# Attention loop of a hybrid attention trunk: the order of the exponential and the copy of the transposed probabilities on ScalarE

## What is computed

```python
def _masked_softmax(s, mask, axis):
    s = jnp.where(mask, s, NEG_INF)
    m = jnp.max(s, axis=axis, keepdims=True)
    e = jnp.where(mask, jnp.exp(s - m), 0.0)
    return e / jnp.maximum(jnp.sum(e, axis=axis, keepdims=True), 1e-30)
...
        ps = _masked_softmax(ss, ms[:, :, None], (-2, -1))
        o_s = jnp.einsum('bgrtkl,bgtkld->btgrd', ps.astype(dt), vs)
...
        pw = _masked_softmax(sw, mw, -1)
        o_w = jnp.einsum('bgrts,bsgd->btgrd', pw.astype(dt), vw)
        return gb[..., 0:1] * o_c + gb[..., 1:2] * o_s + gb[..., 2:3] * o_w
```

## Time and profile before

| what | value |
|---|---|
| median of 3 runs | 2489.19 us (2485.69 to 2492.6) |
| the profiled execution, its own time | 2496.24 us |
| span of its instructions | 2494.1 us |
| mean granted TensorE clock | 0.983 of full speed |
| PE busy | 2335.1 us, 94% of the span |
| ACT busy | 576.9 us, 23% |
| DVE busy | 1435.8 us, 58% |
| POOL busy | 1333.2 us, 53% |

### The profile page before, as it was taken

One profiled execution on the slowest core, in us unless ns is written; L12 is line 12 of the kernel. 1 busy time (PEld: TensorE's weight loads), 2 busy tenths in 40 slices (PEclk: granted clock), 3 DMA queues, 4 the chain that ended last, 5 costly groups with the idle time before them and its releaser, 6 DMA issues.

```text
span 2494.1 us, 36305 instructions
## 1 busy us (share of the span) xinstructions
PE 2335.1 (94%) x12736; PEld 1875.6 (75%) x12736; DVE 1435.8 (58%) x2460; ACT 576.9 (23%) x1114; POOL 1333.2 (53%) x1018
## 2 busy tenths in 40 slices
PE   0798999999999999999998999999999999999996
PEld 0566787877788877777886788787778888787885
DVE  8965654665677775675126155246677776335536
ACT  0211310222233333222024022022232232333001
POOL 6574447544444445555655644654544444554763
PEclk9998999998999999999999999999999999999998
DMA  9855336521122223454315533532222222221532
GB/s 351 307 210 193 121 135 230 172 102 61 67 69 68 72 73 110 155 202 156 100 63 195 197 99 103 184 121 94 69 69 71 73 69 68 69 82 62 193 135 93
DMA packets 94593, 315.92 MB, mean 127 GB/s; under 512 B 10918, under 2 KB 11174, under 8 KB 93382
## 3 DMA queue, kind: packets, MB, share of 16 engines
q1 hardware_dynamic: 86768, 295.46, 34.5%
q10 hardware_dynamic: 7644, 18.16, 2.1%
HBM read 303.86 MB, written 8.39 MB: 125 GB/s over the span
## 4 chain that ended last, share of the span: by engine, by line
PE 70%; DVE 15%; ACT 4%; POOLq 3%; issue 3%; DMA 2%; POOL 2%; DVEq 1%; ACTq 1%; SPq 0%
PE bank L653 14%; PE bank L655 14%; PE bank L654 13%; DVE arena L1715 9%; PE bank L1177 4%; PE bank L1176 4%; PE bank L1175 4%; DVE acc L1715 3%; ACT arena L1205 2%; PE bank L963 2%; PE bank L934 1%; PE bank L617 1%; POOLq L1657 1%; POOL w_lo L1655 1%; DVE tiny L1715 1%
## 5 line engine op out<-in xcount | busy, mean ns | idle before, releaser
L1655 POOL TENSOR_TENSOR w_lo<-ring,w_hi 128x512 fp32r<-128x512 f32 (+1 forms) x632 | 894.5, 1436 | 48.5 <-issue 1.3
L1651 POOL CAST w_hi<-ring 128x1024 fp32r<-128x1024 f32 (+1 forms) x320 | 356.4, 1114 | 1029.9 <-PE bank L655 844.6
L653 PE MATMUL bank<-h_hi,w_hi 128*128 128x512 f32 x1952 | 818.2, 419 | 9.3 <-POOLq L1657 9.3
L655 PE MATMUL bank<-h_hi,w_lo 128*128 128x512 f32 x1952 | 768.3, 394 | 0.0
L654 PE MATMUL bank<-h_lo,w_hi 128*128 128x512 f32 x1952 | 765.5, 392 | 0.0
L653 PEld LDWEIGHTS bank<-h_hi,w_hi 128*128 128x128 f32 x1952 | 370.9, 190 | 91.8 <-issue 15.0
L655 PEld LDWEIGHTS bank<-h_hi,w_lo 128*128 128x128 f32 x1952 | 368.8, 189 | 82.7
L654 PEld LDWEIGHTS bank<-h_lo,w_hi 128*128 128x128 f32 x1952 | 371.0, 190 | 72.5 <-issue 7.2
L1205 ACT ACTIVATE arena<-bank 128x512 f32<-128x512 f32 (+5 forms) x324 | 155.4, 480 | 660.0 <-PE bank L655 217.1
L1715 DVE SCALAR_TENSOR_TENSOR acc<-yT,cact,acc 128x1024 f32<-128x1024 f32 (+1 forms) x144 | 213.2, 1480 | 38.7 <-DMA acc<-in_b_mod 14.7
L1175 PE MATMUL bank<-w_hi,h_hi 128*128 128x512 f32 x448 | 175.7, 392 | 0.8 <-issue 0.8
(11 more groups left out here) (232 smaller groups left out, 2848.0 us busy)
## 6 DMA issues: line engine op xcount, KB each, us to landing
ring<-in_stream SPq DMA_DIRECT2D x352, 512.0 KB, 3.4
yT<-in_stream SPq DMA_DIRECT2D x128, 512.0 KB, 4.6
yT<-in_mod SPq DMA_DIRECT2D x32, 1024.0 KB, 7.8
arena<-in_x ACTq DMA_DIRECT2D x4, 1024.0 KB, 10.3
x_norm<-arena ACTq DMA_DIRECT2D x4, 1024.0 KB, 8.2
arena<-x_norm ACTq DMA_DIRECT2D x4, 1024.0 KB, 10.9
out<-arena SPq DMA_DIRECT2D x3, 1024.0 KB, 3.9
arena<-in_x SPq DMA_DIRECT2D x1, 2048.0 KB, 14.5
```

Source lines behind the costliest of these rows:

```text
L653: mm(PJ[b][:, :], hi, h_hi[:, k, :], start=(k == 0), stop=False)
L655: last = mm(PJ[b][:, :], lo, h_hi[:, k, :], start=False, stop=(k == KT - 1))
L1651: pool.tensor_copy(w_hi[:, par, 0:w], ring[:, slot, 0:w])
L1655: pool.tensor_tensor(w_lo[:, par, at], ring[:, slot, at], w_hi[:, par, at].bitcast(F32), ALU.subtract)
```

## The change

In the loop over the steps of a head, on ACT, the copy of the transposed probabilities of unit s-2 now stands ahead of the exponential of unit s-1. Nothing else differs; the waits, the operands and the semaphores are the same.

```diff
                             if s == 0:
                                 act.wait_ge(S("cmp_scored2"), H + 1)
                                 fn(cmp_s, cmp_s, ACT.Exp).then_inc(S("cmp_exp"), 1)
+                            if 2 <= s <= 9:
+                                u = s - 2
+                                w = (u % TT + 1) * P
+                                act.wait_ge(S("pt_done"), H * 8 + u + 1)
+
+                                act.wait_ge(S("pv_done"), after("pv_done", H * 8 + max(u - 1, 0)))
+                                fn(probT[u % 2][:, 0:w], TB[(u + 1) % 2][:, 0:w], ACT.Copy)\
+                                    .then_inc(S("pt_ready"), 1)
                             if 1 <= s <= 8:
                                 u = s - 1
                                 w = (u % TT + 1) * P
                                 act.wait_ge(S("max_ready"), H * 8 + u + 1)
                                 fn(prob[u % 2][:, 0:w], SB_[(u + 1) % 2][:, 0:w], ACT.Exp, scale=-1.0,
                                    bias=tiny[:, u:u + 1], accum_out=tiny[:, 8 + u:9 + u]).then_inc(S("exp_done"), 1)
-                            if 2 <= s <= 9:
-                                u = s - 2
-                                w = (u % TT + 1) * P
-                                act.wait_ge(S("pt_done"), H * 8 + u + 1)
-
-                                act.wait_ge(S("pv_done"), after("pv_done", H * 8 + max(u - 1, 0)))
-                                fn(probT[u % 2][:, 0:w], TB[(u + 1) % 2][:, 0:w], ACT.Copy)\
-                                    .then_inc(S("pt_ready"), 1)
```

More of the change, by code:

```diff
@@ L1403, in group @@
                                 fn(cmp_s, cmp_s, ACT.Exp).then_inc(S("cmp_exp"), 1)
-                            if 1 <= s <= 8:
-                                u = s - 1
-                                w = (u % TT + 1) * P
-                                act.wait_ge(S("max_ready"), H * 8 + u + 1)
-                                fn(prob[u % 2][:, 0:w], SB_[(u + 1) % 2][:, 0:w], ACT.Exp, scale=-1.0,
-                                   bias=tiny[:, u:u + 1], accum_out=tiny[:, 8 + u:9 + u]).then_inc(S("exp_done"), 1)
                             if 2 <= s <= 9:
@@ L1417, in group @@
                                     .then_inc(S("pt_ready"), 1)
+                            if 1 <= s <= 8:
+                                u = s - 1
+                                w = (u % TT + 1) * P
+                                act.wait_ge(S("max_ready"), H * 8 + u + 1)
+                                fn(prob[u % 2][:, 0:w], SB_[(u + 1) % 2][:, 0:w], ACT.Exp, scale=-1.0,
+                                   bias=tiny[:, u:u + 1], accum_out=tiny[:, 8 + u:9 + u]).then_inc(S("exp_done"), 1)
                             if g == KVH - 1 and r == GROUP - 1 and s == 9:
```

## The result

The changed kernel took 2494.44 us in the median of 20 runs (2489.82 to 2504.59), the kernel before 2490.56 us in 20 runs on the same chip (2484.99 to 2494.81). The ratio is 1.0020 with a 95% interval of 1.0011 to 1.0029: slower by 0.2%, some 5 us, or 3.9 us by the medians. The forecast was 2.8 us slower, 2492.0 us, with 2486 to 2498 as its range and "within 0.3%" as the likeliest case.

The account below looks back on a forecast made before the run. PE, busy 94% of the span, was taken to bound the kernel. Losses of 1.73, 0.98 and 0.05 us summed to 2.8 us, which on the median of 2489.19 us gave 2492.0 us, range 2486 to 2498.

Parts of the forecast that it names:

- The late exponential of unit 1: On ACT in heads 1, 2, 4, 7, 8 and 10: exponential starts later behind the new copy, by 1.22 us in head 1.
- the part of it that DVE's pause eats: In head 1, DVE idles 0.99 us before the minimum of unit 2; 0.90 us of the delay can be absorbed there.
- the 0.3 us that remain at unit 2: In head 1, the 0.32 us left after DVE's pause travels to the scaling and transposes of unit 3.
- the 0.6 us of the copy ahead of unit 3: On ACT in head 3, the copy of unit 2 behind the DMA issues delays the exponential of unit 3 by 0.58 us.
- the zero of heads 5 and 11: In these heads the minimum comes late, not the exponential, so their loss was put at 0.05 us together.
- added clock fall in the heads: Rival: added PE idle time brings one more half-clock stretch; 7.9 us slower in all, 2497.1 us, chance 8%.
- no gain: Rival: PE's waits at L955 charged to ACT were for the moved copy; gain up to 7.3 us, 2481.9 us, chance 4%.
- second pattern: Unit 1 in later heads of a group: late exponential partly reaches PE; heads 1, 2 and 4 lose, sum 0.98 us.
- all late exponentials reach PE: Rival: DVE's pauses cannot absorb the delay, six heads lose 1.22 us each; 9.0 us in all, 2498.2 us, chance 4%.
- first pattern: Step 4 of heads 0, 3, 6 and 9, behind the DMA issues: the copy delays unit 3's exponential; sum 1.73 us.
- The sign that I had named for this pattern: In the profile after, heads 3, 6 and 9: exponential of unit 3 starts 0.6 us behind the end of the DMA issues.
- The bounds, 1.0 to 4.6 us,: Whole kernel: the 2.8 us loss give or take 1.8 us, for DVE durations varying by 0.26 us in 7 heads.

## Why the prediction was right in its verdict and wrong in two terms

**Right.** The page and the views of L955 and L963 named the place: the value products never wait, before or after, so the earlier copy is worth nothing, and all costs are late exponentials that reach PE by way of DVE and L955. The late exponential of unit 1 (1.22 us forecast, 1.21 measured), the part of it that DVE's pause eats, the 0.3 us that remain at unit 2, the gap of 0.09 us behind a copy (0.08 in the row at 284.26), the 0.6 us of the copy ahead of unit 3 (0.62 to 0.63 alone) and the zero of heads 5 and 11 were all borne out. None of the rivals happened: no added clock fall in the heads, no head with the full 1.22 us by way of a pause that could not be eaten, no gain.

**The term of the second pattern, 0.98 us, measured 3.43.** The step that failed is the sentence that the rest, 0.32 us, travels as it is. It assumed that DVE's instructions keep their length when they move. The scaling of unit 2 had 0.38 us of room before POOL's cast; moved by 0.3 it lost the race for it and took 1.34 us for 0.48. The forecast named the cause as an unknown (a scaling of 0.55 or 0.81 us, depending on POOL) and took it for scatter of 0.26 us per head. It is a step: the trace of before had both starts in it, 288.42 and 288.80, and a scaling of 1.34 us at unit 0 of head 3, and a look at POOL's timeline beside DVE's would have shown that 0.38 us was all the room there was, so that the term had a jump close by. But by the records a shift of 0.3 us still leaves 0.09, and that this isn't enough could not be read from them: head 0 with its 0.12 us kept the 0.48. That a start 0.09 us ahead loses only the later runs show. The figure of 1.16 us per head also lies near the rival "all late exponentials reach PE" (1.22), but by another mechanism: delaying DVE alone, with no copy moved, gives the same.

**The term of the first pattern, 1.73 us, measured 0.27.** The failed step is the claim that the exponential of unit 3 starts 0.58 us later because the end of the DMA issues stays where it is. I treated the moved copy only where it arrives and not where it leaves. In step 3 it left a stretch of ACT that was full up to the issues, which then came 0.51 us earlier. With that copy put back the forecast's term appears: 0.42, 0.63, 0.48 and 0.46 us. The sign that I had named for this pattern, an exponential of unit 3 some 0.6 us behind the end of the issues, did come (474.04 for 473.37), and proved nothing, since the issues themselves had moved.

**Heads 7, 8 and 10** lose 0.12 us each where 0 was forecast. The scaling of unit 2 takes 1.34 us there too, but DVE's pause absorbs nearly all of it.

**The bounds, 1.0 to 4.6 us,** held the in-head sum of 4.1, but by luck in part: the two errors, +2.45 and -1.46, have opposite signs. With the second pattern's error alone the sum would have been 5.2, outside. The ratio of the timed runs, 5.0 us slower with an interval of 2.7 to 7.2, doesn't say whether the cost itself lay within them. The waits of L955 are a like case: they grew to 12.5 us where about 12 was forecast, but 3.1 of the 3.3 us are heads 1, 2 and 4, which were to give 1.0.

## What to carry to other kernels

When an edit moves an instruction on an engine that shares something with another, lay the timelines of both engines side by side and note how far each start is from the neighbour's; the effect can be flat up to about that distance and then jump (here between 0.12 and 0.09 us ahead), so a shift must be priced against the room, not carried along by its own length. In an in-order stream, price a moved instruction at both ends: what waits where it arrives, and what comes sooner where it left. And a wait that is taken away counts only after the next place where the engines meet: 1.24 us at the transposes was 0.45 us one instruction group later.

## What the runs showed of the hardware that I had not expected

- A DVE scaling (TENSOR_SCALAR, 128x384, fp32) that starts beside a running POOL cast of 128x1024 ends 0.21 us behind the cast's end, whether it started 0.09, 0.32 or 0.56 us into it (1.16, 0.93, 0.69 us instead of 0.48). Started 0.12 us or more ahead of the cast it keeps 0.48 us (and the cast takes 1.25 us at 0.12, 1.23 at 0.15, 1.04 at 0.38), and started 0.09 us ahead it takes 1.34.
- Beside POOL's cast and split, DVE instructions with two inputs take longer as well: 1.28 to 2.09 or 2.19 us for a multiply-add, 0.68 to 1.60 us for a TENSOR_TENSOR on 32x512.
- The issue of two small DMAs on ACT took 1.16 us in most heads' step 4, but 2.41 us in head 7 and 1.86 us in head 1 of one execution, and 1.83 us in head 4 of another. Why was not tried.
- The fall of the clock behind head 5 differs between two executions of the same kernel (0.78 and 0.93 granted from 562 to 585 us, about 2.9 us of time), so that a pair of profiled spans tells less than the change costs. What sets its length was not tried.
